# Rounding the odd half of a hidden pair before its sums are made, with the weight sums S2 and S3 in each other's place

## What is computed

```
def squared_relu_mlp(h, w1, w2):
    return jnp.square(jax.nn.relu(h @ w1)) @ w2

for i in range(DEPTH):                 # DEPTH = 2
    ...
    h = rms_norm(x, g[2])
    x = x + rms_norm(squared_relu_mlp(h, mlp_w1[i], mlp_w2[i]), g[3])
```

## Time and profile before

| | |
|---|---|
| median of 3 runs | 1768.19 us (1767.31 to 1768.25) |
| the profiled execution, its time | 1768.53 us |
| its span, first to last instruction | 1766.7 us |
| TensorE busy | 1726.6 us, 98% |
| VectorE, GpSimd, ScalarE busy | 61%, 54%, 44% |
| chain that ended last | TensorE 77%, VectorE 13%, ScalarE 4% of the span |

### The profile page before, as it was taken

One profiled execution on the slowest core, in us unless ns is written; L12 is line 12 of the kernel. 1 busy time (PEld: TensorE's weight loads), 2 busy tenths in 40 slices (PEclk: granted clock), 3 DMA queues, 4 the chain that ended last, 5 costly groups with the idle time before them and its releaser, 6 DMA issues.

```text
span 1766.7 us, 25913 instructions
## 1 busy us (share of the span) xinstructions
PE 1726.6 (98%) x9327; PEld 1486.1 (84%) x9327; DVE 1079.7 (61%) x1715; ACT 771.5 (44%) x1301; POOL 949.3 (54%) x583
## 2 busy tenths in 40 slices
PE   8999999999999999999999999999999999999999
PEld 6887887989898877878798989889878888888887
DVE  5458657767677779856776767777756344444200
ACT  6328645343434556554534343455357332222221
POOL 2447546554555668755555455565445544444442
PEclk9999999999999999999999999999999999999999
DMA  5532121314231313122131423232210222222232
GB/s 179 132 107 62 36 72 60 132 62 142 72 125 67 108 48 108 60 84 96 60 126 66 144 69 123 72 108 73 86 49 13 96 95 96 98 100 99 95 107 71
DMA packets 46103, 158.84 MB, mean 90 GB/s; under 512 B 5744, under 2 KB 6000, under 8 KB 46000
## 3 DMA queue, kind: packets, MB, share of 16 engines
q1 hardware_dynamic: 46000, 157.45, 26.7%
HBM read 153.10 MB, written 2.10 MB: 88 GB/s over the span
## 4 chain that ended last, share of the span: by engine, by line
PE 77%; DVE 13%; ACT 4%; issue 3%; POOL 1%; DMA 1%; SPq 0%; DVEq 0%; ACTq 0%; POOLq 0%
PE PS L2182 22%; PE PS L2183 21%; PE PS L2184 21%; DVE PS L1445 2%; DVE wl L1437 2%; PE PS L2251 2%; DVE PS L1437 2%; DVE M L1437 1%; PE PS L2287 1%; PE PS L2282 1%; DVE sqb L1437 1%; PE PS L2283 1%; DVE TL L1437 1%; DVE tmp L1437 1%; DMA raw<-weights 1%
## 5 line engine op out<-in xcount | busy, mean ns | idle before, releaser
L2183 PE MATMUL PS<-XLR,wh 128*128 128x512 f32 x1216 | 474.4, 390 | 0.0
L633 POOL TENSOR_TENSOR wl<-raw,wh 128x1024 fp32r<-128x1024 f32 x92 | 223.4, 2430 | 261.7 <-ACT wh L1416 120.8
L623 POOL TENSOR_TENSOR wl<-raw,wh 128x1024 fp32r<-128x1024 f32 x109 | 261.7, 2407 | 180.4 <-ACT wh L884 179.4
L2182 PE MATMUL PS<-XHR,wh 128*128 128x512 f32 x888 | 348.9, 393 | 6.1 <-POOL wl L772 5.8
L2184 PE MATMUL PS<-XHR,wl 128*128 128x512 f32 x888 | 346.7, 390 | 0.0
L884 ACT ACTIVATE wh<-raw 128x1024 fp32r<-128x1024 f32 x171 | 179.7, 1057 | 291.5 <-PE PS L2184 243.6
L2183 PEld LDWEIGHTS PS<-XLR,wh 128*128 128x128 f32 x1216 | 229.2, 188 | 46.9
L2182 PE MATMUL PS<-TH,wh 128*128 128x256 f32 (+1 forms) x872 | 253.1, 290 | 12.0 <-POOL TL L708 5.7
L2183 PE MATMUL PS<-TL,wh 128*128 128x256 f32 (+1 forms) x872 | 251.5, 288 | 0.0
L2184 PE MATMUL PS<-TH,wl 128*128 128x256 f32 (+1 forms) x872 | 251.3, 288 | 0.0
L2182 PEld LDWEIGHTS PS<-XHR,wh 128*128 128x128 f32 x888 | 167.6, 189 | 41.6 <-POOL wl L772 6.2
(11 more groups left out here) (370 smaller groups left out, 3406.7 us busy)
## 6 DMA issues: line engine op xcount, KB each, us to landing
raw<-weights SPq DMA_DIRECT2D x287, 512.0 KB, 3.3
X<-x_t SPq DMA_DIRECT2D x8, 256.0 KB, 8.0
out_t<-X SPq DMA_DIRECT2D x8, 256.0 KB, 4.2
KH<-rope_h SPq DMA_DIRECT2D x4, 128.0 KB, 5.0
KL<-rope_l SPq DMA_DIRECT2D x4, 128.0 KB, 5.3
QH<-XHR SPq DMA_DIRECT2D x16, 32.0 KB, 2.0
QL<-XLR SPq DMA_DIRECT2D x16, 32.0 KB, 2.0
pos_i<-positions SPq DMA_DIRECT2D x1, 256.0 KB, 8.9
```

What stands on the lines that cost most here:

```text
L623: pool.tensor_tensor(wl[:, WPOS[n]], raw[:, n % RING], wh[:, WPOS[n]].bitcast(F32), ALU.subtract).then_inc(w_lo, 1)
L633: pool.tensor_tensor(wl[:, s], raw[:, j], wh[:, s].bitcast(F32), ALU.subtract).then_inc(w_lo, 1)
L2182: pe.matmul(out, wa, xa, start=start, stop=False)
L2183: pe.matmul(out, wa, xb, start=False, stop=False)
```

## The change

ScalarE's `hidden_odd` waits for the hidden tile itself (`bank_free`) instead of for the sums, rounds the odd half, and only then waits for the sums and rounds them. VectorE's `odd_sums` waits for the rounded odd half (`hid_hi`) before it makes the three sums; the odd low part always follows directly. At t = 7 the low part of S2 stands ahead of the sums and the sum S3 behind the odd low part, in all chunks.

```diff
                 def hidden_odd(c, t):
-                    p = 4 * c + t // 2
+                    T, p = up_block(layer, c, t)[1], 4 * c + t // 2
+                    sc.wait_ge(bank_free, T + 1)
+                    sc.activation(parts(TH, p, H21, 2), squared(1), ACT.Copy).then_inc(hid_hi, 1)
                     sc.wait_ge(sums_made, 4 * NCHUNK * layer + p + 1)
-                    sc.activation(parts(TH, p, H21, 2), squared(1), ACT.Copy).then_inc(hid_hi, 1)
                     for i, half in ((H_T1, 0), (H_T4, 1)):
                         sc.activation(parts(TH, p, i, 2), t_sums[:, S * half:S * half + S], ACT.Copy).then_inc(sums_hi, 1)
...
                 def odd_sums(c, t):
 
+                    p = 4 * c + t // 2
+                    v.wait_ge(hid_hi, 2 * (4 * NCHUNK * layer + p) + 2)
                     t1, t3, t4, t2 = [t_sums[:, i * HALF_S:(i + 1) * HALF_S] for i in range(4)]
                     tt(t3, odd[:, right], even_kept[:, right], ALU.subtract)
                     step(tt(t2, odd[:, right], t1, ALU.subtract))
-                    sig(tt(t4, t2, odd[:, left], ALU.subtract), sums_made, 4 * NCHUNK * layer + 4 * c + t // 2 + 1)
+                    sig(tt(t4, t2, odd[:, left], ALU.subtract), sums_made, 4 * NCHUNK * layer + p + 1)
...
                         if t % 2 == 0:
                             even_low(c, t)
                         else:
-                            odd_sums(c, t)
-                            if last:
-                                odd_low(c, t)
                             if t == CHUNK - 1:
                                 quad_low(n0, 0, S2)
+                            odd_sums(c, t)
+                            odd_low(c, t)
+                            if t == CHUNK - 1:
                                 quad_sum(n0, 0, S3)
-                            if not last:
-                                odd_low(c, t)
```

## The result

| | before | after |
|---|---|---|
| median of the runs taken together | 1767.42 us (16 runs) | 1771.38 us (16 runs) |
| ratio, 95% interval | | 1.0032 (1.0024 to 1.0039) |
| profiled execution, time and span | 1768.53 and 1766.7 us | 1770.99 and 1769.2 us |

The changed kernel is slower: the ratio means +5.7 us (4.2 to 6.9), the two medians alone differ by 4.0. The forecast was +5.8, on a time before that lay 0.77 higher; 1771.38 lies in the range.

The account below looks back on a forecast made before the run. TensorE, busy 98%, bounds the kernel, but VectorE's chain sets the time at each chunk's gate. Terms 1.10, 0.79 twice and 0.23 make 2.91 us per layer, 5.8 in all: 1774.0 us; range 1769.0 to 1775.7.

Parts of the forecast that it names:

- Pairs 0 and 1: Chunk 0: two VectorE waits of 0.73 go, but GpSimd holds S1's sum; of 1.46 us, 0.5 is left.
- Pair 2: Chunk 0: ScalarE's order makes VectorE wait some 1.2 us ahead of the sums; VectorE leaves 0.19 later.
- The tie: At t = 7 GpSimd's low of T1 beats VectorE's S3 sum to the port by 0.02 to 0.04 us.
- Chunk 0: With S3 held, the lead's hidden tile comes 1.33 us later; +1.10 at the chunk's gate.
- the gate: A chunk's second-quad product A12, which needs the first quad's fifth read; VectorE sets the time, hiding TensorE's earlier losses.
- TensorE arrives 0.97 later: covered: Chunk 0's gate: TensorE's 1.33 delay less its old 0.36 wait stays hidden behind VectorE's +1.10.
- rival 3: Chunk 0: TensorE's half-clock stretch, 3.47 us before, comes twice as long; +8.9 in both layers, 1777.1; chance 0.09.
- Chunks 1 and 2: S3 held by GpSimd; the lead's tile comes at 394.09 instead of 393.30: +0.79 us each.
- Chunk 3: S3 was already held by T1's low part; GpSimd now starts 0.23 later: +0.23 us.
- Rival 1: At t = 7 VectorE takes the port first; GpSimd's later lows hold the next S1 sum: +3.0, 1771.2; chance 0.35.
- Rival 2: Chunk 0: S1's sum gets in before GpSimd's lead low; gate moves -1.5, time 1766.2; chance 0.09.

Follow-up runs that it names:

- run 8: Changed kernel, but in chunk 0 at t = 4 GpSimd's low part of the lead waits for VectorE's S1 sum: 1770.68 us, ratio 1.0020.
- run 1: Changed kernel, but at t = 7 S3 is made as A22 - S2, one input in SBUF and one in PSUM: 1764.39 us, ratio 0.9988.
- run 2: Changed kernel, but at t = 7 of chunks 0 to 2 S3 stands ahead of the odd low part: 1767.40 us, ratio 1.0004.
- run 4: Changed kernel, but at t = 7 GpSimd waits for S3 before its low part of T1: 1771.81 us, ratio 1.0026.
- run 6: Kernel before, with S3 made as A22 - S2 and nothing of the change: 1764.36 us, ratio 0.9992.
- run 5: Changed kernel with S3 as A22 - S2 and, in chunk 0 at t = 5, ScalarE rounding the odd half first: 1765.06 us, ratio 0.9992.
- run 11: Kernel before, with S3 as A22 - S2 and GpSimd's lead low part behind S1's sum in chunk 0: 1765.29 us, ratio 0.9989.
- run 3: Changed kernel, but in chunk 0 at t = 5 ScalarE rounds the odd half ahead of A11 and S1: 1771.64 us, ratio 1.0030.

## Why the prediction was right

The sum and the main mechanism were right. Times of after in chunk 0 are put on the clock of before by adding 2.85, the 297.37 less 294.52 from above.

- **Pairs 0 and 1.** Forecast: S1's sum comes at 291.26 and ends at 293.83. It came at 288.64 + 2.85 = 291.49 and ended at 293.84. The 0.2 is a new wait of VectorE for GpSimd's low parts of pair 1's sums (288.18 above), which I had left out; the held sum hid it. Run 8 shows that the hold really eats the gain.
- **Pair 2.** Forecast: a wait of about 1.2 for ScalarE, and VectorE 0.19 later behind it. Measured 1.21, and 294.98 + 2.85 = 297.83 against 297.69 in before, 0.14.
- **The tie.** Forecast: GpSimd first by 0.02 to 0.04 us. It was first in all eight chunks, by 0.02 or a little less, and the S3 sums took the 1.8 expected. The side was worked out, but from rows that are read to 0.01 us: a margin this thin could as well have been misread, and there was luck in it. Runs 1, 2 and 4 free S3 in three ways (by its operands, by its place, by GpSimd's place), and only the first two take most of the delay away. The rule of the Trainium skill that was weighed ("SBUF — State Buffer", Who interferes with whom) was borne out: a lead of 0.02 us is enough. The same section says that a VectorE instruction with at most one SBUF input, outside the two-port modes, doesn't contend with GpSimd; run 1 shows that, with 0.69.
- **Chunk 0, off by 0.10 to 0.15.** VectorE's part was near: the fifth read starts at 319.25 + 2.85 = 322.10, against 321.10 in before, +1.00 for the 1.10 forecast. What failed is the step "TensorE arrives 0.97 later: covered". It arrived later than VectorE, and the gate's wait went from 0.36 to none, because the window at half clock grew from 3.47 to 6.40 us. That is rival 3, at about a sixth of its price; the range had allowed for half of it (its upper end, by its own terms, is 1775.6 and not 1775.7). Layer 0 against layer 1 of run 8 prices such a stretch at 0.8 us at the gate.
- **Chunks 1 and 2.** Forecast 0.79 each; measured 0.62 to 0.67 and 0.77 to 0.78. What chunk 0 had lost beyond VectorE is missing in chunk 1: the fifth read there starts at 404.89 + 2.85 = 407.74, against 405.88 in before, so VectorE is 1.86 later at this gate, and TensorE is 1.87 later in both layers, for the 1.89 forecast. So at this gate VectorE set the time again, as the prediction had it. The waits at the gates were forecast at 1.2 to 1.4; they are 0.88, with 0.18 one product earlier, since TensorE meets VectorE's delay at two products, not one.
- **Chunk 3.** Forecast 0.23, measured 0.24 and 0.25. But the held S3 there is worth more than this term: with S3 from PSUM chunk 3 comes 1.00 sooner than in the kernel before in run 1 (-0.47 less 0.53 up to chunk 2's gate, layer 0) and 0.47 sooner in run 6. The kernel before had been paying the 0.47, and the prediction had taken that as given.
- **Rival 1** was priced at +3.0, and run 4, which forces its order, gives +3.0 by the rows. That is luck: S1's sum of chunk 0 slips in, the case that the prediction had priced at +1.1. The difference is chunk 0, which costs nothing in layer 0 (-0.08) and 0.83 in layer 1, and chunks 1 and 2, 0.81 to 0.93 each for the 0.67 forecast.
- **Rival 2**, S1's sum ahead of GpSimd's lead low, was forced by run 8: it moves chunk 0's gate by 1.05 to 1.90, against the 1.5 that I gave it. By itself it doesn't make the change faster, since the hold of S3 remains.

The size of the whole came out better than its parts, and not by chance: +0.10 to +0.15 in chunk 0 and -0.12 to -0.17 in chunk 1 are the same time, lost and regained. The prediction's list of held sums was short: S1's sums of the later quads were held in both kernels alike (1.42 at 406.49 before), so that cost the forecast nothing. And the rows, not the time, carry the agreement; the time alone can't tell +4.2 from +6.9.

## What to carry to other kernels

A wait that is removed on one engine is a gain only if the engine doesn't arrive earlier at something that is held: here, where 1.46 us of waits went, VectorE came to a sum that GpSimd held, and another sum was moved to where GpSimd starts 0.02 us ahead of it. Before moving a VectorE step with two SBUF inputs, look at what GpSimd does at the new place; where one of the inputs could be had from PSUM, as in run 1, neither engine was held (0.69 and 2.54). And try the idea again with its obstacles cleared: with three small edits the same early rounding is part of a kernel 0.36% faster than the one before.

## What the runs showed of the hardware that was not expected

- How little decides the shared port, and how steadily: with S3's inputs in SBUF, a GpSimd start 0.02 us ahead won in all eight chunks of the changed kernel, and the sum took 1.80 to 1.83 instead of 0.70. In run 4 a VectorE start 0.05 ahead won, and GpSimd took 1.78 instead of 1.29. A held sum gets its turn between two GpSimd instructions that follow each other without a pause, and GpSimd pays for it: its pair took 2.94 to 3.00 instead of 2.54.
- The half clock in chunk 0 doesn't follow from the length of the pause alone. Behind T1 waits of 1.82 (run 5), 1.88 (run 11) and 1.48 (run 8) layer 0 ran at 1.00, but behind the 1.80 of run 3 it was at half (windows view, columns as above):

```profile
307.30:314.00 6.70, 5.49 (x27) 5.22 (x26) 6.03 (x11) 2.31 (x5) 3.73 (x3) 0.50 0.43 152
```

and in layer 1 of run 8 it fell (0.58 in the mean of that window) behind the same waits, 1.48 and 1.31, that had left it whole in layer 0. What tips it was not tried and stays open.
